# Dense gate table built in rounds of 96 tokens instead of pairs of 48-token blocks, in a hybrid decoder step with a PEER expert layer

## The reference, cut to what matters

```
q  = (x @ w_q) per head and half;  s = q . sub_keys        # 8 heads, 2 halves, 128 keys each
top 16 of each half -> 256 sums -> top 16 -> expert index = 128*i + j, gates = softmax(sums)
y  = sum over heads and picks of  gate * gelu(x . u_tab[index]) * v_tab[index]
```

## Time and profile before

| | us |
|---|---|
| median of 3 runs | 4609.78 (4591.53 to 4627.65) |
| profiled execution, own time | 4625.82 |
| its span | 4624.0 |
| PE busy | 4403.2 (95%) |
| DVE busy | 3029.6 (66%) |
| POOL busy | 2166.4 (47%) |
| ACT busy | 1128.4 (24%) |

### The profile page before, as it was taken

The page is one execution under the profiler, slowest core; times in us unless marked ns, Lnnn a source line. Parts: engine busy times, 40 slices in busy tenths (PEclk is TensorE's granted clock), DMA queues, the critical chain, the costliest instruction groups (busy, mean ns, idle before and its releaser), DMA issues. The chain is left out here.

```text
span 4624.0 us, 75363 instructions
## 1 busy us (share of the span) xinstructions
PE 4403.2 (95%) x28709; PEld 4301.5 (93%) x28709; DVE 3029.6 (66%) x5421; ACT 1128.4 (24%) x2077; POOL 2166.4 (47%) x1529
## 2 busy tenths in 40 slices
PE   7999999999999999999999899978999999999998
PEld 6999999999879999998999889978999999999998
DVE  5124550011236673445788989969998898999998
ACT  3111331111223331023222234322122121222122
POOL 2233232233213222342355478856666676766664
PEclk9999999999999999999999999999999999999999
DMA  5122222433452114444222189999999999999997
GB/s 189 55 59 74 92 96 93 120 110 95 151 171 57 50 42 153 140 123 125 79 78 81 61 309 361 358 331 317 340 327 331 316 329 328 330 347 347 346 330 243
DMA packets 578544, 911.58 MB, mean 197 GB/s; under 512 B 150536, under 2 KB 398344, under 8 KB 578245
## 3 DMA queue, kind: packets, MB, share of 16 engines
q1 hardware_dynamic: 430016, 422.36, 28.5%
q0 software_dynamic: 111744, 406.90, 24.8%
q10 hardware_dynamic: 36640, 80.36, 4.8%
HBM read 775.67 MB, written 133.84 MB: 197 GB/s over the span
## 5 line engine op out<-in xcount | busy, mean ns | idle before, releaser
L2811 PE MATMUL ea_banks<-h_high,ea_uT_high 128*128 128x336 f32 x2048 | 657.1, 321 | 23.7 <-ACT ea_coef L3734 14.5
L2811 PE MATMUL ea_banks<-h_high,ea_uT_low 128*128 128x336 f32 x2048 | 652.9, 319 | 0.0
L2811 PE MATMUL ea_banks<-h_low,ea_uT_high 128*128 128x336 f32 x2048 | 649.1, 317 | 0.0
L123 PE MATMUL p_in<-h_high,w_in_high 128*128 128x352 f32 x1536 | 496.0, 323 | 0.0
L123 PE MATMUL p_in<-h_low,w_in_high 128*128 128x352 f32 x1536 | 492.3, 321 | 0.0
L123 PE MATMUL p_in<-h_high,w_in_low 128*128 128x352 f32 x1536 | 492.1, 320 | 0.0
L2811 PEld LDWEIGHTS ea_banks<-h_high,ea_uT_high 128*128 128x128 f32 x2048 | 388.9, 190 | 25.1 <-ACT ea_coef L3734 14.8
L2786 POOL DMA_INDIRECT ea_u_raw<-in_peer_v,gt_index x192 | 292.3, 1522 | 249.0 <-DVE h_low_plain L3849 188.9
L2786 POOL DMA_INDIRECT yT<-in_peer_u,gt_index x256 | 329.1, 1286 | 139.3 <-issue 48.9
L2811 PEld LDWEIGHTS ea_banks<-h_low,ea_uT_high 128*128 128x128 f32 x2048 | 388.5, 190 | 0.0
L2811 PEld LDWEIGHTS ea_banks<-h_high,ea_uT_low 128*128 128x128 f32 x2048 | 387.5, 189 | 0.0
(11 more groups left out here) (558 smaller groups left out, 11416.1 us busy)
## 6 DMA issues: line engine op xcount, KB each, us to landing
w_in_raw<-in_w_in SPq DMA_DIRECT2D x88, 512.0 KB, 3.8
ex_gate<-tmp_gates SPq DMA_DIRECT2D x64, 672.0 KB
ea_u_raw<-in_peer_uT SPq DMA_DIRECT2D x66, 512.0 KB
w_mb_raw<-in_peer_v SPq DMA_DIRECT2D x64, 512.0 KB
ea_uT_low_plain<-in_peer_uT SPq DMA_DIRECT2D x62, 512.0 KB
ex_lv_low_plain<-in_peer_v SPq DMA_DIRECT2D x62, 512.0 KB
tmp_acts<-ea_coef ACTq DMA_DIRECT2D x64, 336.0 KB
tmp_gates<-yT SPq DMA_DIRECT2D x28, 768.0 KB
```

The costliest lines, as they stand in the source:

```text
L123: last = pe.matmul(banks[0:rows, n, 0:CH], a[:, kk, 0:rows], b[:, kk, chunk(n)], start=(kk == 0 and a is wt.high[s] and b is high), stop=( ...
L2811: last = pe.matmul(acts.banks[:, n, 0:CD], a[:, c, :], b[:, c, dense(n)], start=(c == 0 and a is acts.uT_high[s] and b is high), stop=(c = ...
```

## The change

GATE_BLOCK goes from 48 to 96. The table lies in 7 blocks of 96, so one gate load is 7 x 128 runs of 768 bytes. `out` is now cut by tiles (HALF = 64) in place of tokens: each buffer holds 64 tiles x 96 tokens, the same bytes, and each unit writes both, in two copies. A round still has 24 units and 4 tiles, but the first tile is done whole (both chunks) before the first unit, and the other three have a chunk before every fourth unit (0, 4, ..., 20). ACT waits once a round, before the first unit's copies, for the stores of both buffers. SP issues the four stores of a round (1536 KB each) together once the last unit of the round has been kept, and after them the four u loads. 36% of a round's dots stand in the first three units.

```
-GATE_BLOCK = 48
+GATE_BLOCK = 96
-    units = 2 * BT // UN
-    rounds = blocks // 2
+    units = BT // UN
+    rounds = blocks
-    per_chunk = units // (TILES * DC)
-    PARTS, STORE_AT = 4, (0, 3, 5, 7)
+    per_chunk = units // ((TILES - 1) * DC)
+    PARTS = 4
+    HALF = P // 2
+    AHEAD = 0.36
...
+        def dots_by(i, r):
+            done = AHEAD * (r + 1) / SLOTS if r < SLOTS else AHEAD + (1 - AHEAD) * (r + 1 - SLOTS) / (units - SLOTS)
+            return P if (i, r) == (rounds - 1, units - 1) else int(P * (i + done) / rounds)
...
 DVE, in a round
-                    if r % (per_chunk * DC) == per_chunk:
+                    if r == 0 or r % (per_chunk * DC) == per_chunk:
                         (cut_u of the next tile)
...
 PE, a round
+                e, half, s = tile_of(i, 0)
+                for n in range(DC):
+                    act_chunk(pe, acts, high, low, e, s, n)
                 for r in range(units):
                     if r % per_chunk == 0:
-                        j, n = r // per_chunk // DC, r // per_chunk % DC
+                        j, n = 1 + r // per_chunk // DC, r // per_chunk % DC
...
 ACT
-                act.copy(out[r * UN // BT][:, :, at:at + UN], ps[:, r % SLOTS, :, :].rearrange("p n i -> p i n")).then_inc(kept, 1)
+                for hf in range(2):
+                    last = act.copy(out[hf][:, :, at:at + UN], ps[:, r % SLOTS, :, hf * HALF:(hf + 1) * HALF].rearrange("p n i -> p i n"))
+                last.then_inc(kept, 1)
...
+                raise_u(act, acts, e + 1, half + s, 1 - s)
+                for n in range(DC):
+                    gelu_chunk(act, acts, tmp, e, half, s, n)
...
-                    if r * UN % BT == 0 and not first:
-                        act.wait_ge(stored[r * UN // BT], 16 * PARTS * i)
+                    if r == 0 and not first:
+                        for hf in range(2):
+                            act.wait_ge(stored[hf], 16 * (PARTS // 2) * i)
...
 SP
+            def store_round(i):
+                sp.wait_ge(kept, units * (i + 1))
                 for q in range(PARTS):
+                    hf, at = q // 2, q % 2 * (HALF // 2)
+                    part = slice(q * P // PARTS, (q + 1) * P // PARTS)
+                    sp.dma_start(tmp["gates"][ds(i, 1), :, part, :].rearrange("o j i n -> j (o i) n"),
+                                 out[hf][:, at:at + HALF // 2, :]).then_inc(stored[hf], 16)
+            def load_tiles(i):
+                for j in range(TILES):
+                    next_u(sp, acts, io, ROUTE_TILES + 2 + TILES * i + j, j % 2)
+            load_tiles(0)
             with sp.Fori(1, rounds) as i:
+                store_round(i - 1)
+                load_tiles(i)
+            store_round(rounds - 1)
```

More of the change, by code:

```diff
@@ L3294, in spread_gates @@
     assert blocks * BT == ND and TILES * rounds == SPREAD_TILES
-    per_chunk = units // (TILES * DC)
-    PARTS, STORE_AT = 4, (0, 3, 5, 7)
-    assert PARTS == TILES
+    per_chunk = units // ((TILES - 1) * DC)
+    PARTS = 4
+    HALF = P // 2
+    AHEAD = 0.36
     with ExitStack() as ctx:
@@ L3306, in spread_gates @@
         free = room[:, :, :].rearrange("q c n -> q (c n)")
-        out = [free[:, 0:P * BT].rearrange("q (i n) -> q i n", i=P), sb("out1", [P, P, BT])[:, :, :]]
+        out = [free[:, 0:HALF * BT].rearrange("q (i n) -> q i n", i=HALF), sb("out1", [P, HALF, BT])[:, :, :]]
         spare = 3 * (NT - G) * P
-        row = [free[:, P * BT + r * D:P * BT + (r + 1) * D] for r in range(2)]
+        row = [free[:, HALF * BT + r * D:HALF * BT + (r + 1) * D] for r in range(2)]
         row += [picks[:, spare + r * D:spare + (r + 1) * D] for r in range(2)]
@@ L3312, in spread_gates @@
         ps = ctx.enter_context(nc.psum_tensor("sg_ps", [P, SLOTS, UN, P], F32))
-        now = ctx.enter_context(nc.psum_tensor("sg_now", [P, 2, 2 * BT], F32))
+        now = ctx.enter_context(nc.psum_tensor("sg_now", [P, 2, BT], F32))
         h_row = ctx.enter_context(nc.psum_tensor("sg_h", [P, D], F32))
@@ L3324, in tile_of, with dots_after @@
             return ROUTE_TILES + TILES * i + j, ROUTE_TILES // 2 + TILES // 2 * i + j // 2, j % 2
-        def dots_after(n):
-            return range(P * n // (units * rounds), P * (n + 1) // (units * rounds))
+        def dots_by(i, r):
+            done = AHEAD * (r + 1) / SLOTS if r < SLOTS else AHEAD + (1 - AHEAD) * (r + 1 - SLOTS) / (units - SLOTS)
+            return P if (i, r) == (rounds - 1, units - 1) else int(P * (i + done) / rounds)
+        def dots_after(i, r):
+            return range(dots_by(i, r - 1) if r else (dots_by(i - 1, units - 1) if i else 0), dots_by(i, r))
         @block.gpsimd
@@ L3342, in _ @@
                     pool.tensor_tensor(first_key, first_key, over_columns(chosen[:, 2, at:at + UN]), ALU.mult).then_inc(hot_weighed, 1)
-                    for m in dots_after(i * units + r):
+                    for m in dots_after(i, r):
                         if m + RING < P:
@@ L3360, in round_of @@
                     dve.wait_ge(hot_made, units * i)
-                dve.tensor_copy(now[:, :, :], chosen[:, 0:2, ds(i * 2 * BT, 2 * BT)]).then_inc(now_made, 1)
+                dve.tensor_copy(now[:, :, :], chosen[:, 0:2, ds(i * BT, BT)]).then_inc(now_made, 1)
                 dve.wait_ge(now_made, i + 1)
@@ L3370, in round_of @@
                     dve.tensor_tensor(keys[s], all_keys, own_keys, ALU.is_equal).then_inc(hot_made, 1)
-                    if r % (per_chunk * DC) == per_chunk:
-                        e, half, s = tile_of(i, r // (per_chunk * DC))
+                    if r == 0 or r % (per_chunk * DC) == per_chunk:
+                        e, half, s = tile_of(i, r // (per_chunk * DC) + 1 if r else 0)
                         cut_u(dve, acts, e + 1, 1 - s)
@@ L3375, in round_of @@
                         dve.wait_ge(h_here, 1)
-                    for m in dots_after(units * i + r):
+                    for m in dots_after(i, r):
                         dot(m)
@@ L3410, in keep @@
                 act.wait_ge(spread, units * i + r + 1)
-                at = r * UN % BT
-                act.copy(out[r * UN // BT][:, :, at:at + UN], ps[:, r % SLOTS, :, :].rearrange("p n i -> p i n")).then_inc(kept, 1)
+                at = r * UN
+                for hf in range(2):
+                    last = act.copy(out[hf][:, :, at:at + UN], ps[:, r % SLOTS, :, hf * HALF:(hf + 1) * HALF].rearrange("p n i -> p i n"))
+                last.then_inc(kept, 1)
             def round_of(i, first=False):
+                e, half, s = tile_of(i, 0)
+                raise_u(act, acts, e + 1, half + s, 1 - s)
+                for n in range(DC):
+                    gelu_chunk(act, acts, tmp, e, half, s, n)
                 for r in range(units):
                     if r % per_chunk == 0:
-                        j, n = r // per_chunk // DC, r // per_chunk % DC
+                        j, n = 1 + r // per_chunk // DC, r // per_chunk % DC
                         e, half, s = tile_of(i, j)
@@ L3435, in _ @@
             sp.dma_start(gt.x2T, tmp["x2T"][:, :, 0:GT]).then_inc(x2_in, 16)
[L3436 to L3442, removed]
-                for q in range(PARTS):
[L3445 to L3454, removed]
+            def store_round(i):
+                sp.wait_ge(kept, units * (i + 1))
+                for q in range(PARTS):
+                    hf, at = q // 2, q % 2 * (HALF // 2)
[6 more added lines that the diff above has]
+            load_tiles(0)
             with sp.Fori(1, rounds) as i:
[L3456 to L3459, removed]
+                store_round(i - 1)
+                load_tiles(i)
+            store_round(rounds - 1)
             sp.wait_ge(x2_in, 16)
-    return [(stored[bs], 16 * PARTS * rounds) for bs in range(2)]
+    return [(stored[hf], 16 * (PARTS // 2) * rounds) for hf in range(2)]
 def experts(nc, k, io, tmp, high, low, yT, acts, wt, gt, gates_stored):
```

## The result

The changed kernel takes 4685.15 us (median of 4 runs, 4678.22 to 4693.06) against 4600.65 (4 runs, 4572.18 to 4627.65) beside it: ratio 1.018, 95% interval 1.014 to 1.022. It is 84.5 us slower; forecast were 61, a time of 4671 and a range of 4595 to 4740. The profiled execution took 4685.07 us, span 4683.0.

The account below looks back on a forecast made before the run. PE, DVE and DMA were taken to lie within a few per cent of each other in both stages. Burst +96, stage end +9 and gates -44 gave +61 us on a median of 4609.8, so 4671; range 4595 to 4740.

Parts of the forecast that it names:

- The burst: Spread stage: PE stands 15 us before unit 3 while ACT waits for the stores; +16 us a round, six times, +96.
- released by ACT's copy in each of six rounds: Spread stage sign: PE idle 10 to 20 us before unit 3 in each of six rounds, ended by ACT's copy.
- The cover: Spread stage: three chunks and three units, 14.3 us, run during the stores; without them the stall would be that much longer.
- Round 0: First round of the spread stage: waits for no store, so no loss was counted.
- The end of the stage: Spread stage's last four stores, 1536 KB in place of 768, delay the first gates and rows: +9 us (7 to 11).
- The gates: Experts stage: gate loads in 768-byte runs save 1.46 us of DMA time a turn, 30 turns, -44 us (0 to -71).
- The sum: Whole kernel: 96 + 9 - 44 = +61 us, giving a median of 4671.
- Not slower: Rival: burst lands at about 20 us and experts' turns all reach 44.74 us; sum -3, 4607; chance 0.30.
- Nothing for the experts: Rival: experts stage gains nothing from longer runs; 96 + 9 = +105, 4715; chance 0.17.
- Even sharing of rows and stores: Rival, spread stage: all 8 rows get through before the last store, landing at 30 us; +93, 4703; chance 0.11.

Follow-up runs that it names:

- e5: Changed kernel with tile 2's load ahead of the four stores and 12.5% of a round's dots early in place of 36%: ratio to before 1.018, rounds 70.6 us.
- e8: Changed kernel with chunks before every third unit, as in the kernel before, and no first tile done whole: ratio to before 1.016, rounds 70.3 us.
- e12: Changed kernel with chunks before every third unit, no first tile done whole, and 12.5% early dots: one run, 4667.06 us, rounds 68.7 us.
- e1: Kernel before, with only its gate loads changed to read the same bytes in runs of 768 bytes: 4579.21 us, ratio to before 0.996.
- e2: Changed kernel with its gate loads reading the same bytes in runs of 384 bytes: ratio to before 1.028, turns 47.4 us.

## Why the prediction was right

**The burst.** Mechanism, place and sign were right, and the round's extra 18.5 us stand against 16 forecast. PE's waits grew by 15.2 us a round, where a stall of 15 was forecast, and its busy time by 3.2, where 2 were forecast for the clock. Inside that, the landing was taken at 25 us and was mostly 21 to 23 (20.5 to 24 after the burst's first issue, in e5, e8 and e12): the engines ran at 390 GB/s in the burst, not at the 371 of the row used. In the round shown the copy came at 24.7, not 29. What filled the gap back up was a lock that the prediction did not have: it counted the early rows as traffic that delays the stores, and not as work that DVE must finish before key 2. PE restarted 27.2 us after the last copy, at unit 2, with one unit more to do; 27.2 + 40.3 + 2 = 69.5, and the 3 us up to 72.7 are short waits and longer busy time. In the two rounds that ACT ended, PE restarted 27.5 and 27.1 us after the burst's first issue. That the size of the stall came out so close is in part luck: an earlier copy, and a second lock and short waits that the sum did not have, made up for each other. The sign "released by ACT's copy in each of six rounds" held in two.

**The cover.** "Without the 14.3 us of cover the stall would be that much longer" was wrong. e8 has 10.5 us of cover and a shorter round, since the lone tile also puts tile 2's load in front of ACT's first copy. The step that was wrong is that cover and wait were taken as independent.

**Round 0** was taken at nothing ("moving dots changes no count"); it lost 5 us, to the early dots.

**The end of the stage.** +9 forecast, +6 measured: twice the bytes landed in 18.0 us, not 19.8.

**The gates.** -44 forecast. The trace of the profiled pair says -62, e1 says -22 (7 to 33) and e2 52. The cost of a run of 768 bytes, worked out in the way of the forecast, came out at 34 ns, as taken. By the overhead that the Trainium skill gives in "DMA: Bandwidth & Descriptors", "Why small descriptors are slow (HBM only)", the forecast had noted 10% less for the same bytes; the traces have 24 ns for 384 bytes and 34 for 768, 29% less, and the measurement decides. What was mis-sized is how engine time turns into turn time: in these traces it is no proportional share but a matter of how many turns are at the floor.

**The sum.** 96 + 9 - 44 = 61 against 84.5 in the medians: the burst 15 larger, round 0 another 5, the end 3 smaller. The stage's start was 1 us earlier. What is left of 84.5 for the experts is -37, by subtraction and not measured, and not the -62 of the profiled pair, since the profiled execution of before was a long one.

**The rivals.** Not slower: ruled out by the 14 us stalls; it needed the copy at 24 us or earlier and the rows out of the way. Nothing for the experts: ruled out by e1 and e2. Even sharing of rows and stores: its time, with eight rows through before the last store, did not come. Its rule did. The DMA queues of the changed kernel from 2815 to 2825, in the middle of a burst (SP's stores, then the rows):

```profile
q1 hardware_dynamic: 241, 2.76, 70.2%
q0 software_dynamic: 240, 0.92, 22.4%
```

Both queues moved the same number of packets, while a store's packet carried up to 12 KB and a row's 4 KB. That agrees with the Trainium skill ("DMA: Bandwidth & Descriptors", "Queues, rings and completion order"), by which an engine goes round its queues packet by packet. The rival's count of rows was wrong: POOL asked for four rows between 2808.94 and 2813.68, the four slots of the ring, and for the next one only at 2822.31, when a dot was done. Four rows and one activation store beside 6.29 MB are 8.7 MB, 22 us at 390 GB/s. In that window the rows got a third of the bytes that SP's queue moved, and DVE waited for them until 2828.97.

## What to carry to other kernels

Joining two half-size buffers that took turns into one that is filled, flushed and waited for whole turns a steady transfer into a burst. Price it as bytes over the full DMA rate, with the other queues' bytes added, against the work that can go on meanwhile, and look for everything that stands in the waiting engine's order or behind the burst in its queue: removing one of two locks that open at nearly the same time gave almost nothing here (rounds of 71.9 and 74.0 us against 72.7). When longer runs are what is wanted, try the order of the table in memory first; it gave a gain here (31 us in the medians) without touching the schedule.

## What the runs showed of the hardware

In the experts stage turns are either at 44.75 us, to within 0.02 for up to 27 in a row, or scattered around 47.5, with nothing between for long. The eleven kernels with 768-byte loads had 15 to 28 of 31 turns at the floor, the two with 384 bytes 5 and 7, the one with 5376 bytes 10. What tips a kernel from one into the other within a run stays open. Two queues that both had work moved packets one for one (241 and 240 in 10 us), so the queue with the larger packets got the larger share of the bytes. Stores of 384 bytes at a pitch of 768, 16384 of them a round, cost no time that a round shows (54.0 us against 54.2), with the DMA share up from 0.96 to 1.08; where the stores were waited for, at the stage's end, they took 4 us longer.
